# Expert rows gathered and summed in a new order, the first experts opened feature tile by feature tile, and the Fourier weights folded into the transform's tables

## What is computed

```python
def moe(h, ...):                     # top-4 of 32 clamped SwiGLU experts
    weights = softmax(top_k(h @ w_router + b_router, 4))
    gate, up = split(xblk @ w_gu[e] + b_gu[e])
    act = (clip(up, -7, 7) + 1.0) * min(gate, 7) * sigmoid(1.702 * min(gate, 7))
    y[token] += weight * (act @ w_down[e] + b_down[e])
h = rmsnorm(h + g2 * moe(...), final_norm_w)

def fourier_attention_layer(x, ...):
    f_in, f_gate, q, k, v, a_gate = split(rms_norm(x, norm_g) @ w_in)
    fmix = fftn(f_in by 4 groups of 256, axes=(sequence, channel)).real
    fmix = einsum('bsgc,gce->bsge', fmix, fourier_w)     # 256 x 256 per group
    f_out = fmix * silu(f_gate)
```

## Time and profile before

| | |
|---|---|
| median of 3 runs | 2349.99 us (2348.99 to 2350.17) |
| the profiled execution | 2349.28 us |
| its span, first to last instruction | 2347.0 us |
| PE busy | 2210.5 us, 94% |
| DVE, ACT, POOL busy | 33%, 20%, 6% |
| mean granted clock of TensorE | 0.976 |
| HBM read and written | 539.58 and 25.03 MB |

### The profile page before, as it was taken

The page is one execution under the profiler, slowest core; times in us unless marked ns, Lnnn a source line. Parts: engine busy times, 40 slices in busy tenths (PEclk is TensorE's granted clock), DMA queues, the critical chain, the costliest instruction groups (busy, mean ns, idle before and its releaser), DMA issues. The chain is left out here.

```text
span 2347.0 us, 35635 instructions
## 1 busy us (share of the span) xinstructions
PE 2210.5 (94%) x14438; PEld 905.5 (39%) x14438; DVE 780.9 (33%) x1411; ACT 470.0 (20%) x837; POOL 144.8 (6%) x174
## 2 busy tenths in 40 slices
PE   5999886999999999999999983999999998999998
PEld 2434541333333333333333321455445444444443
DVE  1133447522222222222222244003077003456543
ACT  2121222111011111001111102110126002446530
POOL 0000002101111101111101031000000000000000
PEclk9999997999999999999999996999999999999999
DMA  9138528999999999999999984113210221122210
GB/s 364 54 114 308 210 95 338 391 414 417 416 416 415 416 414 417 417 416 414 415 416 416 415 306 165 54 54 101 89 54 1 72 72 45 54 90 90 72 36 36
DMA packets 144126, 557.13 MB, mean 237 GB/s; under 512 B 19397, under 2 KB 34926, under 8 KB 110178
## 3 DMA queue, kind: packets, MB, share of 16 engines
q1 hardware_dynamic: 118998, 513.20, 55.4%
q0 software_dynamic: 11472, 30.31, 3.6%
q10 hardware_dynamic: 13596, 12.80, 1.6%
HBM read 539.58 MB, written 25.03 MB: 241 GB/s over the span
## 5 line engine op out<-in xcount | busy, mean ns | idle before, releaser
L1952 PE MATMUL ps<-ring,xeT 128*32 128x512 f32 x6144 | 669.6, 595 | 4.9 <-ACT xeT L1553 4.9
L1952 PEld LDWEIGHTS ps<-ring,xeT 128*32 128x32 f32 x6144 | 196.3, 110 | 450.6 <-issue 444.1
L1922 PE MATMUL ps<-ring,mT 128*32 128x512 f32 x2048 | 267.9, 595 | 8.1 <-DVE mT L1762 8.1
L1672 ACT ACTIVATE mT<-mT 128x768 f32<-128x768 f32 x32 | 27.0, 843 | 898.6 <-DVE mT L1748 898.6
L1748 DVE TENSOR_SCALAR mT<-ps 128x768 f32<-128x768 f32 x32 | 30.6, 957 | 488.8 <-PE ps L1952 488.8
L360 PE MATMUL ps<-hT_late,ring 128*128 128x512 f32 x384 | 167.6, 599 | 4.5 <-PEq L2218 4.5
L1930 PE MATMUL ps<-ring,mT 128*32 128x256 f32 x2048 | 157.7, 380 | 0.0
L1930 PEld LDWEIGHTS ps<-ring,mT 128*32 128x32 f32 x2048 | 66.3, 110 | 154.7 <-issue 154.7
L2897 PE MATMUL ps<-hT_late,ring 128*128 128x512 f32 x256 | 110.6, 592 | 1.3 <-PEq L2656 1.3
L360 PEld LDWEIGHTS ps<-hT_late,ring 128*128 128x128 f32 x384 | 73.8, 193 | 97.5 <-issue 97.5
L360 PE MATMUL ps<-ring,mT 128*128 128x512 f32 x256 | 110.1, 592 | 1.2 <-PEq L2463 1.2
(11 more groups left out here) (399 smaller groups left out, 2038.9 us busy)
## 6 DMA issues: line engine op xcount, KB each, us to landing
ring<-in_w_gu SPq DMA_DIRECT2D x256, 1024.0 KB, 8.6
ring<-in_w_down SPq DMA_DIRECT2D x128, 1024.0 KB, 7.9
ring<-in_even_w_in SPq DMA_DIRECT2D x18, 1024.0 KB, 7.4
ring<-in_w_ada SPq DMA_DIRECT2D x32, 512.0 KB, 6.4
ring<-in_odd_w_in SPq DMA_DIRECT2D x32, 512.0 KB, 5.4
ring<-in_w_ada SPq DMA_DIRECT2D x8, 1024.0 KB, 20.8
ring<-in_w_in SPq DMA_DIRECT2D x8, 1024.0 KB, 15.3
y_scratch<-ysb ACTq DMA_DIRECT2D x128, 64.0 KB, 4.7
```

The costliest lines, as they stand in the source:

```text
L1672: nc.scalar.activation(sig[:, 0:W], gate[:, 0:W], ACT.Sigmoid, scale=1.702).then_inc(M.sig_ready, 1)
L1922: mm = nc.tensor.matmul(quad(b, 2 * q + n), acted(k, q, src), w[:, kk, n * BANK:(n + 1) * BANK], start=first, stop=last)
L1952: mm = nc.tensor.matmul(quad(q, c), left(q), part_columns(w, c), start=start, stop=stop)
```

## The change

Six things change together.

1. In the opening, ACT writes the token table; DVE works out the places of the first two experts alone and the rest while the first gather is under way; it turns the gathered rows before it makes the next list of ids. PE waits for the feature tiles of the first two experts one by one (`opening=True`). ACT scales the inputs of the second expert ahead of the first one's sigmoid.
2. The row buffers are six, and experts 0 to 28 count as early. The first four sums stand inside expert 30's DVE work, the other twelve ahead of the last expert's; there is one more set of four fetches, for expert 29.
3. The last rows (expert 31) are fetched in the norm block, and the four sums of expert 30 stand there too. `w1b` is loaded long before.
4. SP stores the third part of y for the last two experts.
5. `fourier_w` is multiplied into the cosine and sine tables by 64 matmuls in the norm block (`dcw`), ahead of the transposes; the Fourier block then has no matmuls with the weights. The Nyquist column is made by 256-column matmuls, then transposed.
6. ACT's features and DVE's scaling of `res` move past the barrier into the Fourier block; the product with the gate moves past the next one (`mixed`).

```diff
-        stream.turn(LATE_SLOTS)
+        stream.turn(LATE_SLOTS, 2)
         w_even = A["even_w_in_2"][0]
+        add(rows(A["dft_c"]), 2, 512)
+        add(A["fourier_w_2"][0].rearrange("g (k p) n -> p (g k) n", p=P), 8, 256)
...
-        BEFORE = E - 2
+        gbuf = [buf[:, 2 * b:2 * b + 2, :].rearrange("p k n -> p (k n)") for buf, b in
+                [(hT, b) for b in range(4)] + [(mT, KD // 2 + 1), (mT, KD // 2 + 3)]]
+        GB = len(gbuf)
+        BEFORE = E - 3
...
+                stream.load(sp, end_moe - 7)
+                sp.wait_ge(parted.sem, 4)
+                w1b_loaded.on(sp.dma_start(w1b, A["final_norm_w"].rearrange("(a n) -> a n", a=1).to_broadcast([P, D])), 16)
+                for e in (E - 2, E - 1):
+                    sp.wait_ge(M.y_read, e + 2)
+                    for c in range(4):
+                        part = slice(c * QUAD, (c + 1) * QUAD)
+                        sp.dma_start(y_rows(e, 2, 4, c), ysb[part, Q2]).then_inc(M.y_stored, 16)
                 stream.load(sp, end_moe)
...
+                for n in range(NT * TOPK + 2 * NT):
+                    i, t = divmod(n - NT * TOPK, NT)
+                    after = max(i, -1) + 1
+                    if n == 0 or n >= NT * TOPK and t == 0:
+                        pool.wait_ge(M.y_stored, 128 * (BEFORE + 1 + after))
                     if n >= GB:
                         pool.wait_ge(row_used.sem, n - GB + 1)
...
                 def block_step(e, first, last=False):
+                    if first:
+                        act.wait_ge(M.gate_done, 1)
+                        act.wait_ge(M.xT_done, 2)
+                        act_modulate(act, M)
                     act.wait_ge(M.gu_read, e * 2 + 1)
...
-                    if not last:
+                    if not (first or last):
                         act.wait_ge(M.xT_done, e + 2)
                         act_modulate(act, M)
...
-                split_places(list_step, posm[:], place[:], third_of[:])
+                split_places(list_step, posm[:, :, 0:2], place[:, :, 0:2], third_of[:, :, 0:2])
...
-                with dve.Fori(0, E - 3) as i:
+                with dve.Fori(0, E - 4) as i:
...
-                sum_rows(0, 2 * TOPK)
+                bias_added.wait(dve)
+                prepare(E - 2)
+                block_step(E - 2, False, between=lambda: sum_rows(dve, 0, TOPK))
+                sum_rows(dve, TOPK, NT * TOPK)
                 block_step(E - 1, False, last=True)
-                sum_rows(2 * TOPK, 3 * TOPK)
+                sum_rows(dve, NT * TOPK, NT * TOPK + NT)
                 dve.wait_ge(M.y_done, 2 * (E - 1))
                 read_y(E - 1, Y0)
-                sum_rows(3 * TOPK, NT * TOPK)
                 dve.wait_ge(M.y_done, 2 * E)
                 read_y(E, Y0 + 2)
-                sum_rows(NT * TOPK, NT * TOPK + NT)
...
                     for k in range(KD):
                         w = tile(m0 + k, turn)
+                        if opening:
+                            pe.wait_ge(M.xeT_read, e * 8 + k + 1)
                         mm = gate_up(lambda q: xeT[:, k, q * QUAD:(q + 1) * QUAD], w, k == 0, False)
...
+                sum_rows(dve, NT * TOPK + NT, NT * TOPK + 2 * NT)
+                row_used.wait(dve)
                 w1b_loaded.wait(dve)
                 join(0)
...
+                for i, j in enumerate(j_dw):
+                    m, g = i % 2, i // 2
+                    j.open(pe)
+                    for s in range(2):
+                        for kk in range(2):
+                            mm = nc.tensor.matmul(ps[:, j.bank, s * 256:(s + 1) * 256],
+                                                  dc[:, kk, s * 256 + m * P:s * 256 + (m + 1) * P], fw[:, 2 * g + kk, :],
+                                                  start=kk == 0, stop=kk == 1)
+                    j.done(mm)
...
-                for i, j in enumerate(j_fw):
-                    g, e = i // 2, i % 2
-                    if i in (0, 4):
-                        j_sq[i // 4][3].emptied_for(pe)
-                    j.open(pe)
-                    for kk in range(2):
-                        mm = nc.tensor.matmul(bank(j.bank), fw[:, 2 * g + kk, e * P:(e + 1) * P], fT[:, 2 * g + kk, :],
-                                              start=kk == 0, stop=kk == 1)
...
+                mixed.on(nc.vector.tensor_tensor(mT[:, 0:KD, :], mT[:, 0:KD, :], fT, ALU.mult))
```

More of the change, by code:

```diff
@@ L1650, in _ @@
             def _(act):
+                for q in range(3):
+                    tokens_ready.on(nc.scalar.copy(tokens[:, :, 2 * q:2 * q + 2],
+                                                   cst[:, C_TOK:C_TOK + 2 * NT].rearrange("p (t c) -> p t c", t=NT)))
                 nc.scalar.copy(ysb[:, 0:1], ident[:, 0:1]).then_inc(M.y_read, 1)
@@ L1676, in block_step @@
                     if not first:
-                        store(e)
+                        store(e, third=not last)
                 def store(e, third=True):
@@ L1953, in gate_up, with block_step @@
                     return mm
-                def block_step(e, m0, turn, first, second=False, last=False):
-                    pe.wait_ge(M.xeT_read, e * 8 + 8)
+                def block_step(e, m0, turn, first, opening=False, second=False, last=False):
+                    if not opening:
+                        pe.wait_ge(M.xeT_read, e * 8 + 8)
                     if not first:
@@ L2260, in _ @@
                 scale(3)
-                for t in range(NT):
-                    nc.vector.tensor_scalar(res[:, t, :], hw[:, t, :], pair[:, t, 2:3], None, ALU.mult)
             @block.scalar
@@ L2286, in _ @@
                 pe.wait_ge(M.y_read, E + 1)
+                dc, fw = take(pe), take(pe)
+                for i, j in enumerate(j_dw):
[7 more added lines that the diff above has]
+                    j.done(mm)
+                for _ in range(2):
+                    stream.owe()
                 for t in range(NT):
@@ L2339, in _ @@
             def _(dve):
+                for t in range(NT):
+                    h_ready.on(nc.vector.tensor_scalar(res[:, t, :], hw[:, t, :], pair[:, t, 2:3], None, ALU.mult))
                 for half in range(2):
@@ L2387, in _ @@
                     pe.wait_ge(folded.sem, 4 * half + 4)
+                    if half:
+                        j_nt.open(pe)
+                        for c in range(2):
+                            mm = nc.tensor.transpose(ps[:, j_nt.bank, c * P:(c + 1) * P], nyrow[:, c * P:(c + 1) * P], ident)
+                        j_nt.done(mm)
                     for (s, t), j in j_ch[half].items():
```

184 lines of the change are left out of this document (93 added, 91 removed).

## The result

The changed kernel takes 2323.76 us (median of 4 runs, 2322.59 to 2325.52) against 2349.49 us for the kernel before in the same job (2348.97 to 2350.17): a ratio of 0.9891, 95% interval 0.9874 to 0.9908. It is faster, as forecast, but by 25.7 us instead of 36, and the time lies above the range given. The profiled execution took 2324.58 us with a span of 2322.7 us.

The account below looks back on a forecast made before the run. PE was taken to be busy almost throughout, so only its waits, half-clock stretches or less work could pay. 0.5 - 23.9 - 12.8 = -36.2 us gave 2313.5 us, range 2306 to 2322.

Parts of the forecast that it names:

- Part 1: Opening of the experts: PE gains 1.1 us, a 5.2 us pause costs 1.6 us of clock; sum +0.5 us.
- the step on the sigmoid: Opening: sigmoid done 5.1 us after the gate's end, against 1.9 before; DVE, waiting for it, loses 2.2 us.
- Part 2: End of the experts to the Fourier block: projection starts at 1432.2 instead of 1456.12, sum -23.9 us.
- At 6.8 us a fetch and six buffers they come every 1.7 us at worst: End of the experts: pace of the last twelve of sixteen rows, 20 us from 1358, done at 1378.
- under the same load: Argument against the slower rival: the four fetches of 1369.57 landed back to back under the same load.
- No row here shows both queues full for long: Remark on late weights: the profile rows given show no long stretch with both DMA queues full.
- the stores: End of the experts: 9.8 us from reading expert 30's y to POOL's next fetch, 2 us less with SP sharing.
- The block ends 3.1 us behind its last one: End of the experts' block: POOL's last fetch at 1402.1, block end 3.1 us later, at 1405.2.
- The rest of part 2: Norm block: first join at 1412.4, not waiting for a DMA, projection at 1432.2.
- Part 3: Fourier block: the 32 weight matmuls of 13.90 us go, next projections start at 1600.3 instead of 1613.11; sum -12.8 us.
- Slower than before: Rival, 3%: in expert 30, starved fetches come one by one at 6.8 + 1.3 us and PE waits for DVE; 2397.
- Weights come late: Rival, 10%: fetches crowd the weight transfers, PE waits 3 to 8 us in experts 30 and 31; 2317 to 2323.

Follow-up runs that it names:

- Run 8: Changed kernel, but ScalarE takes the first expert's sigmoid ahead of the two feature scalings again, as the kernel before did: 2320.49 us.
- run 7: Changed kernel, but DVE adds the second half of the down bias (`add_bias(1)`) before the building of positions: 2318.13 us.
- run 2: Changed kernel with four row buffers instead of six: 2327.44 us.
- run 3: Changed kernel, but each of the first sixteen row fetches brings 512 of 1024 columns, from other rows of the table: 2314.49 us.
- run 4: Changed kernel, but the last expert's gate stands ahead of the last four of sixteen sums, and expert 30's y is read ahead of expert 29's four sums: 2323.4 us.
- Runs 6: Changed kernel, but SP's last loads stand behind the barrier of the experts' block instead of ahead of it: 2324.34 us.
- 10: Changed kernel with second bias half early, last gate ahead of four sums, two tiles instead of four ahead of the stores, remaining tiles after the last rows: 2309.28 us.
- runs 5: Kernel of run 4, but two of the next stage's four tiles are asked for behind the last stores: 2322.78 us.
- 11: As run 10, but SP asks for the even projection's first tiles at the start of the norm block, not behind the last four rows: 2314.52 us.
- 12: As run 10, but the last gate is behind all sixteen sums and expert 30's y is read behind expert 29's four sums: 2314.37 us.

## Why the prediction was wrong

**Part 1 held.** Forecast: starts early, a stall of 5.2 us ahead of the first down product, 1.6 us of clock, +0.5 in all. Measured: 5.00 us, 0.55 behind it for 3.4 us, +1.0. Run 8 confirms the step on the sigmoid, and run 7 that `add_bias(1)`, at the end of DVE's chain, is what holds PE: without the stall the opening gives some 7 us.

**Part 2 failed, -11.3 us for -23.9.** The step that failed is "At 6.8 us a fetch and six buffers they come every 1.7 us at worst". It divides the latency of one fetch by the number of buffers. In the changed kernel the rows are fetched for 50 us beside a full weight queue, and get the packets' share of a bandwidth that does not grow: a row in 2.7 us beside the down weights, in some 3.9 us beside the gate/up weights with their larger packets. The latency follows from the pace (13.8 us, about five rows in flight) and not the other way round; fewer buffers leave the pace alone (run 2), fewer bytes raise it (run 3).

The prediction also took the 6.8 us as measured "under the same load", and the trace of before does not bear that out. The queues in its windows 1370 to 1376 and 1376 to 1381:

```profile
q1 hardware_dynamic: 349, 1.30, 54.1%
q0 software_dynamic: 311, 1.13, 47.4%
...
q0 software_dynamic: 283, 0.97, 59.9%
```

For 6 us the rows shared the bandwidth nearly packet for packet; then SP's queue, which had nothing more to load, ran dry (there is no q1 in the second window), and the four rows finished alone. "No row here shows both queues full for long" is true of the rows shown, but these 6 us could have been looked up: 1.13 MB in 6 us is one row in 2.7 us.

**What the step cost.** To the projection's start part 2 gained 8.9 us (1446.73 against 1456.12, less the 0.5 us that the stages ahead had gained), 15.0 less than forecast. The block's end hangs on expert 30's y, which DVE reads behind the sums and the last gate. That reading ended at 1402.4, where 1389.1 was forecast: with the 0.5 us, 13.8 of the 15.0 us. (PE's last down product came 11.5 us late in the same way, with its stall and 10.2 us at the half clock, but run 4 shows that PE was not what the block waited for.) The other terms nearly cancel: +4.0 behind POOL's last fetch, -2.4 for the stores, -0.4 for the rest. The projection then ran 2.4 us faster, which leaves 12.6.

**The step behind it was mis-sized too.** "The block ends 3.1 us behind its last one" was 7.13 us. The row of before was measured with SP silent; in the changed order SP's loads start at 1411.9, together with the fetches. Runs 6 and 10 show 2.96 and 2.84 us without them. The stores took 5.4 us instead of the 7.8 forecast; the 9.8 us of before from which that was worked out were no store time, since POOL's fetch at 1411.81 waited for DVE to free a row buffer.

**The rest of part 2 held**: from the first join to the projection 19.5 us, forecast 19.8, and the join waits for no transfer. One gain was not seen: the projection runs in 110.10 us instead of 112.52, with a granted clock of 1.00 at its start instead of 0.50. That the joined weights keep PE busy in the norm block is not enough to explain it: runs 5, 10, 11 and 12 have them too, and there the projection starts at 0.50 and takes 112.1 to 112.5 us. The cause stays open, and these 2.4 us brought the time nearer to the forecast by luck.

**Had only the last gate come in time, nothing would have been gained.** Run 4 takes the stall away and the time stays, since the stores then queue beside the projection's weights (14.9 us). In run 3 expert 30's y is read at the same point, to within a microsecond, and the next fetch follows 8.1 us behind; it has taken nearly 4 MB out of the queues. That this is why it reaches the forecast is read from the two traces and was not tested by itself. The prediction treated the bandwidth as a matter of weights arriving late for PE. It was the row and store transfers behind the weights that arrived late, for DVE and POOL.

**Part 3 held**: -12.8 us, forecast -12.8, and term by term, so it was no luck. The table products, the sequence transform with its 257th column (13.98 us) and the barrier came as worked out. Behind the barrier, 1.91 us of idling brought a half clock for 3.4 us, some 1.7 us, that the prediction did not have; it falls behind the point up to which the 12.8 us are counted, and the rest of the program is 0.3 us longer in all.

**The rivals.** "Slower than before", at 3%, had the mechanism, fetches starved by a full weight queue, against 2.9 us a row that DVE could afford; the sixteen rows took 53.9 us from the first fetch to the last sum, 3.4 us each. At that pace it cost most of the gain at the experts' end, and not the whole of the change. "Weights come late" had the right resource and the wrong victim. In the changed kernel PE waits for no weight tile for longer than a matmul's gap, and expert 30 takes 1.2 us longer than the one before it (33.1 against 31.9). The Trainium skill (DMA: Bandwidth & Descriptors, "Queues, rings and completion order") says that each engine takes turns between its queues, packet by packet. The trace agrees, with 557 packets against 561 in 10 us. By that rule the rows' pace could have been estimated ahead: half of the measured 410 GB/s is one row of 0.5 MB in 2.4 us, not 1.7. The prediction used the rule for the weights and did not apply it to the rows.

## What to carry to other kernels

Where transfers run at full bandwidth already, work out a new stream's pace from its share of the packets and what they carry, not from the latency of a single transfer in a quieter stretch; then ask for every transfer in that stretch what queues behind it. Before a latency is carried over from a trace, look at what the other queues moved in just those microseconds. Taking a stall away pays only up to the next wait that ran beneath it: here the gate's order was worth nothing until the loads were moved. A prefetch that nobody needs for 40 us belongs behind the small transfers that the path waits for.

## What the hardware showed unasked

- Two full queues shared by packets, even when these carried different amounts: 557 packets with 1.87 MB beside 561 with 2.15 MB from 1370 to 1380, and 234 with 0.77 MB beside 232 with 1.73 MB from 1344 to 1350. The queue with the larger packets got more of the bandwidth.
- A few small fetches were held up by bulk loads of another queue: the last four fetches of the block, whose queue moves 0.19 MB, kept POOL 7.13 us in the changed kernel, and 5.1 to 8.3 us in all runs in which SP's loads follow; without them it is 2.8 to 3.1 us (runs 6, 10, 11, 12 and the kernel before).
- A store of 0.4 MB beside full queues took 14.9 us from the end of the reading to the next fetch (run 4), though ACT had issued its four of the eight parts in 1.8 us; in the changed kernel it took 5.4.
- Idle time of 1.91 us ahead of matmuls was enough for a half clock at 1589.1, while 2.21 us ahead of the first down product in run 8 was not. Nor is it the length of the gap: 1.13 us ahead of the first projection went with 1.00 in the changed kernel and with 0.50 in runs 5, 10, 11 and 12. What decides stays open.
